# Identity passes on TensorE in the opening and ahead of the last mixer, and ScalarE's, VectorE's and TensorE's steps of the mixers in another order

## The reference

```python
cs = silu(c)
mod = (cs @ ada_w[l] + ada_b[l])                      # 9 x 1024 values for each l
x = x + 0.5 * gate0 * swiglu(norm(x), ...)
x = x + gate1 * mixer(norm(x), ...)                   # convolution + dilated attention, 3 x 8 heads
x = x + 0.5 * gate2 * swiglu(norm(x), ...)
```

```python
q, k, v, xr, xg = split(u @ w_in)
hr = rg_lru(causal_conv(xr), ...)                     # r, ig = sigmoids; a = exp(..); scan over time
y_a = (hr * gelu(xg)) @ w_lru_out
y_b = swa_sink_attention(q, k, v, sinks, bias) @ w_attn_out
g = sigmoid(u @ w_gate + b_gate)                      # two gates, g0 and g1
h = h + norm((g0 * y_a + g1 * y_b) @ w_o)
```

## Time and profile before

| | |
|---|---|
| median of 3 runs | 2094.27 us (2092.14 to 2094.92) |
| the profiled execution | 2095.6 us, of which 2093.5 us are the span of its instructions |
| TensorE matmul / weight load | 2059.9 us (98%) / 1790.4 us (86%) |
| VectorE / ScalarE / GpSimd | 1432.5 us (68%) / 1028.6 us (49%) / 36.3 us (2%) |
| HBM read | 435.05 MB, 208 GB/s over the span |
| granted clock, mean | 0.997 of full speed |

### The profile page before, as it was taken

One profiled execution on the slowest core, in us unless ns is written; L12 is line 12 of the kernel. 1 busy time (PEld: TensorE's weight loads), 2 busy tenths in 40 slices (PEclk: granted clock), 3 DMA queues, 4 the chain that ended last, 5 costly groups with the idle time before them and its releaser, 6 DMA issues.

```text
span 2093.5 us, 28979 instructions
## 1 busy us (share of the span) xinstructions
PE 2059.9 (98%) x11649; PEld 1790.4 (86%) x11649; DVE 1432.5 (68%) x1822; ACT 1028.6 (49%) x1279; POOL 36.3 (2%) x78
## 2 busy tenths in 40 slices
PE   7999999999999999999999999999999999999998
PEld 7788888999888888888899998888788799998887
DVE  5887788668777677767866786455654669656454
ACT  4443544444554363445444445444644668646443
POOL 0000000000000000000000000000000010000000
PEclk9999999999999999999999999999999999999999
DMA  9787698447678748868865496654755454456652
GB/s 316 258 283 251 193 290 253 128 139 253 230 256 267 245 168 277 264 202 260 287 183 145 143 300 192 203 188 141 234 188 183 135 160 137 161 183 210 192 190 80
DMA packets 355929, 438.04 MB, mean 209 GB/s; under 512 B 9571, under 2 KB 323371, under 8 KB 355796
## 3 DMA queue, kind: packets, MB, share of 16 engines
q1 hardware_dynamic: 350592, 420.51, 61.7%
q0 software_dynamic: 4160, 14.23, 3.1%
q10 hardware_dynamic: 1044, 1.46, 0.2%
HBM read 435.05 MB, written 1.11 MB: 208 GB/s over the span
## 4 chain that ended last, share of the span: by engine, by line
PE 88%; DVE 5%; ACT 4%; issue 1%; DMA 1%; DVEq 1%; SPq 0%; ACTq 0%
PE PC L1808 7%; PE PC L1810 7%; PE PC L1809 7%; PE PA L1808 6%; PE PA L1810 6%; PE PA L1809 6%; PE PB L1808 6%; PE PB L1810 6%; PE PB L1809 6%; PE PA L1801 4%; PE PA L1802 4%; PE PA L1803 4%; PE PC L1839 3%; PE PC L1976 2%; PE PC L1801 2%; PE PC L1803 2%
## 5 line engine op out<-in xcount | busy, mean ns | idle before, releaser
L1172 DVE TENSOR_TENSOR lo<-raw,hi 128x2048 fp32r<-128x2048 f32 x274 | 626.7, 2289 | 209.5 <-ACT hi L696 208.4
L696 ACT ACTIVATE hi<-raw 128x2048 fp32r<-128x2048 f32 x277 | 529.3, 1912 | 260.1 <-PE PC L1810 114.8
L1198 DVE SCALAR_TENSOR_TENSOR acc<-raw,cs,acc 128x256 f32<-128x256 f32 x448 | 217.2, 485 | 34.4 <-issue 0.9
L1808 PE MATMUL PA<-hi,nn 128*128 128x512 f32 (+1 forms) x528 | 210.3, 398 | 7.0 <-DVE nn L1274 5.9
L1801 PE MATMUL PA<-nn,hi 128*128 128x256 f32 x720 | 209.0, 290 | 0.4 <-ACT f L1089 0.4
L1810 PE MATMUL PA<-hi,nn 128*128 128x512 f32 (+1 forms) x528 | 206.0, 390 | 0.0
L1809 PE MATMUL PA<-lo,nn 128*128 128x512 f32 (+1 forms) x528 | 205.5, 389 | 0.0
L1802 PE MATMUL PA<-nn,lo 128*128 128x256 f32 x720 | 203.6, 283 | 0.0
L1803 PE MATMUL PA<-nn,hi 128*128 128x256 f32 x720 | 203.6, 283 | 0.0
L1808 PE MATMUL PB<-hi,nn 128*128 128x512 f32 x400 | 158.2, 395 | 0.5 <-DVE nn L1274 0.5
L1810 PE MATMUL PB<-hi,nn 128*128 128x512 f32 x400 | 156.6, 391 | 0.0
(11 more groups left out here) (317 smaller groups left out, 4088.8 us busy)
## 6 DMA issues: line engine op xcount, KB each, us to landing
raw<-in_w_in SPq DMA_DIRECT2D x90, 1024.0 KB, 5.4
raw<-in_ada_w SPq DMA_DIRECT2D x66, 1024.0 KB, 7.4
raw<-in_ffn_w_gate SPq DMA_DIRECT2D x88, 512.0 KB, 4.1
raw<-in_ffn_w_up SPq DMA_DIRECT2D x88, 512.0 KB, 5.2
raw<-in_ffn_w_down SPq DMA_DIRECT2D x44, 1024.0 KB, 5.2
raw<-in_ffn_w SPq DMA_DIRECT2D x88, 512.0 KB, 4.8
raw<-in_ffn_w SPq DMA_DIRECT2D x22, 1024.0 KB, 4.8
raw<-in_w_o SPq DMA_DIRECT2D x12, 1024.0 KB, 6.6
```

Of the source, the lines that this page charges most:

```text
L696: A(parts_of(n)[0], raw[:, n % 3, :], ACT.Copy).then_inc(hi_done, 1)
L1172: V.tensor_tensor(l, raw[:, n % 3, :], h.bitcast(F32), ALU.subtract).then_inc(lo_done, 1)
L1198: i = V.scalar_tensor_tensor(o, w[:, k, :], cs[:, k:k + 1], o, ALU.mult, ALU.add)
L1808: MM(o, xl, wh[:, c0:c0 + w], start=first, stop=False, skip_group_check=True)
```

## The change

- TensorE: a function `warm(n, bank)` multiplies the 128x128 identity by the identity repeated four times (512 columns, fp32), n times, into a bank that nothing reads. In the opening stand 4 behind the first matmul, 3, 1, 1 and 1 in the rounds n = 1, 2, 3 and 4 of the loop over VectorE's five units, and 1 behind `turn_x(0, 1)`, eleven in all; 2 more stand ahead of `values2(0, 7)`, the start of the last mixer.
- TensorE, first-kind mixers: the first scores (j = 0, u = 0) wait for 11 sums of queries and keys instead of all 12, the ones of u = 1 for all 12.
- ScalarE, last mixer: on even hu, `split` comes ahead of `gate2`; the last square root, `lru(3, 1)`, comes behind the split of its hu and ahead of the gate.
- TensorE, last mixer: `first_unit` also waits for `sg_done` 18.
- VectorE: at the change of stage 5 the split comes ahead of `final_norm(0)`; behind the last mixer's loop `lru(3, 3)` comes ahead of `split(b + 19)`.

```diff
--- before.py
+++ after.py
@@ -1137,7 +1137,7 @@
                     recurrent_gates(j)
                 if i == 3 and 1 <= j < 4:
                     lru(j - 1, 2)
-                if i == 0 and j >= 1:
+                if i == 0 and 1 <= j < 4:
                     lru(j - 1, 1)
                 if i == 4 and 0 <= j < 4:
                     lru(j, 0)
@@ -1145,9 +1145,11 @@
                     after(b + 3 + u)
                     if SPREAD[u] == "q":
                         queries(u // 3 + 1, prod[(u + 1) % 2])
-                    elif SPREAD[u] in ("ga", "gc"):
+                    split(b + 6 + u)
+                    if i == 0 and j == 4:
+                        lru(j - 1, 1)
+                    if SPREAD[u] in ("ga", "gc"):
                         gate2(f1 if SPREAD[u] == "ga" else f2, SPREAD[u], 0, prod[1])
-                    split(b + 6 + u)
                 if i == 1 and j == 4:
                     lru(j - 1, 2)
 
@@ -1337,8 +1339,8 @@
                 elif s == 5:
                     add_gated(s, 0)
                     midway()
+                    split(BASE[s + 1])
                     final_norm(0)
-                    split(BASE[s + 1])
                     lows(Aq, 0, (0,))
                     add_gated(s, 1, (0,))
                     lows(Aq, 0, (1,))
@@ -1778,8 +1780,8 @@
                     chunk_T(8 + c, c, oH2, oL2)
 
             def last_chunks():
+                lru(3, 3)
                 split(b + 19)
-                lru(3, 3)
 
             tail(7, TAIL_AT2 + 3, TAIL2[3:], BANK2[3:], gate_home2, mH2, mL2, m322, ya2, False, 8, 19, last_chunks,
                  None)
@@ -2063,6 +2065,15 @@
             pe.wait_ge(const_done, 8)
             pe.wait_ge(c_full, 16)
             MM(PA[:, 512:512 + KC], crow[:, :], ident[0:KC, 0:KC], start=True, stop=True).then_inc(c_turned, 1)
+            wide_ident = bass.AP(ident[:, :].tensor, ident[:, :].offset, [ident[:, :].ap[0], [0, 4], [1, P]])
+
+            def warm(n, bank):
+
+                for _ in range(n):
+                    MM(bank.rearrange("p (e q) -> p e q", e=4), ident[:, :], wide_ident, start=True, stop=True,
+                       skip_group_check=True)
+
+            warm(4, PC[:, 1024:1536])
             pe.wait_ge(cs_done, 1)
 
             def rows_turned():
@@ -2086,15 +2097,22 @@
                     ada_cols_of(1)
                     rows_turned()
                 if n == 1:
+                    warm(3, PC[:, 1024:1536])
                     ada_cols_of(3)
+                if n == 2:
+                    warm(1, PC[:, 1024:1536])
                 if n == 3:
                     turn_x(0, 0)
                     ada_cols_of(6)
+                    warm(1, PC[:, 1024:1536])
+                if n == 4:
+                    warm(1, PC[:, 1024:1536])
                 pe.wait_ge(ada_d, n + 1)
                 for c in (2 * u, 2 * u + 1):
                     i = MM(MOD[:, c:c + 1], acc[:, c * P:(c + 1) * P], ones[:, 0:1], start=True, stop=True)
             i.then_inc(mod_done, 1)
             turn_x(0, 1)
+            warm(1, PA[:, 512:1024])
 
             def bias_lines():
 
@@ -2138,8 +2156,8 @@
                         half(c + u, prod[u], 0, nh, nl)
                         if u == 0 and j:
                             chunk_T(l * 4 + j - 1 if j > 1 else None, (j - 1) % 2, st0 + 4 * j)
-                        if j == 0 and u == 0:
-                            pe.wait_ge(qk_done, 12 * (l + 1))
+                        if j == 0 and u < 2:
+                            pe.wait_ge(qk_done, 12 * l + 11 + u)
                         tick(1, st0, 4 * j, 2 * u, v1, l * 4 + j if j else None)
                         half(c + u, prod[u], 1, nh, nl).then_inc(unit_done, 1)
                         tick(1, st0, 4 * j, 2 * u + 1, v1)
@@ -2167,6 +2185,7 @@
                              k == 0, k == KC - 1)
                 return m
 
+            warm(2, PB[:, 0:512])
             values2(0, 7)
             turn_x(7, 1)
             values2(1, 7).then_inc(unit_done, 1)
@@ -2222,6 +2241,7 @@
 
             def first_unit(k, o):
                 pe.wait_ge(ol_done, 16)
+                pe.wait_ge(sg_done, 18)
                 unit(k, o, oH2, oL2)
 
             def first_recurrent(k, o):
```

## The result

The changed kernel takes **2099.12 us** (median of 7 runs, 2098.70 to 2102.57). The kernel before took 2093.28 us beside it (7 runs, 2092.14 to 2094.92). The ratio is 1.0031 with a 95% interval of 1.0021 to 1.0040, that is 4.4 to 8.4 us slower. The profiled execution took 2099.1 us with a span of 2097.3, against 2095.6 and 2093.5 before: 3.8 us of span.

A forecast was written before the change was run, and what follows sets the result against it. TensorE, 88% of the chain, was taken as the bound: only its idle time or lower clock could matter. Terms 2.0 - 1.3 + 0 - 0.9 + 2.8 + 2.0 = +4.6 on 2094.27 gave 2098.9 us, range 2092.5 to 2105.0.

The forecast's parts named there:

- The opening: Eleven passes in the opening: clock rises, falls in one-column groups, single passes don't restore it; +2.0 us (bounds -0.8, +9.2).
- My mark: Opening: the prediction is wrong if the one-column groups take under 4 us each.
- The first-kind mixers: Earlier first scores remove the 1.08 us key-sum wait; 0.63 us earlier each, twice: -1.3 us (bounds 0, -2.2).
- VectorE's split ahead of the norm: Change of stage 5: norm ends later, but TensorE waits for VectorE a little behind anyway; 0 us (bounds 0, +1.5).
- The two passes: Start of last mixer: they fill a 2.0 us wait and keep the clock; -0.9 us (upper bound +1.9).
- The last mixer's order: ScalarE's new order and first_unit's wait: TensorE idles 5.2 us, partly given back; +2.8 us (bounds +2.0, +3.0).
- The clock behind the idle stretch: Last mixer: TensorE's clock falls behind the 5.2 us without matmuls; +2.0 us (bounds 0, +2.9).
- The carry-over to the median: Whole kernel: the profiled execution lies 1.3 us above its median, so +4.6 was applied to 2094.27 us.
- A: Rival: the clock holds through the opening, -0.8 us there instead of +2.0; total 2096.1 us; chance 0.25.
- B: Rival: fp32 identity passes don't raise the clock, so the opening costs the full +9.2; total 2106.1 us; chance 0.13.
- C: Rival: last mixer's sigmoid is done when TensorE asks (before 1801.4); with the opening at -0.8, 2091.3 us; chance 0.10.
- D: Rival: all gaps and gains over the whole kernel cancel, 2094.3 us; chance 0.05.

The follow-up runs named there:

- experiment 1: Kernel before with only the eleven passes of the opening added: 2096.54 us, ratio 1.0014.
- experiment 5: Changed kernel with TensorE's wait for sg_done 18 moved from first_unit to first_recurrent: 2096.56 us, ratio 1.0009 to the kernel before.
- experiment 7: Kernel before with eight of the opening's eleven passes (4, 3 and the last 1), without the three single ones between: 2094.06 us, ratio 1.0007.
- experiment 8: Kernel before with only the three single passes of the opening, ahead of the last one-column groups: 2097.95 us, ratio 1.0018.
- experiment 4: Kernel before with only the two passes ahead of the last mixer: 2093.79 us, ratio 1.0001.
- experiment 10: Kernel before with only VectorE's two swaps (split ahead of the final norm; lru(3, 3) ahead of split(b + 19)): 2091.97 us, ratio 0.9994.
- experiment 3: Kernel before with only the last mixer's new ScalarE and VectorE order and first_unit's wait for sg_done 18: 2099.88 us, ratio 1.0030.
- experiment 9: Kernel before with only ScalarE's split ahead of the first gate's sigmoid in the last mixer: 2096.10 us, ratio 1.0011.

## Why the prediction was right, and where it wasn't

The forecast was 2098.9 us and the result is 2099.12. That they meet within 0.2 us is partly luck. The forecast was +4.6 on a median of 2094.27; the kernel before had 2093.28 in the comparison, and the change came out at +5.8. And some of the terms were off, in both directions.

**The opening, forecast +2.0.** Line 1216 was to start at 41 and starts at 42.3: +3.4 in the trace, +3.0 in experiment 1. The picture held: the passes at 2.5 us and the three ahead of the second group raise the clock, it falls at such groups (once in the idle stretch behind the first, once inside the second), single passes don't bring it back in this execution, and the last passes are paid in full. The price of a pass held as well: 1.85 us at 1.2 GHz (forecast 1.8), about 0.9 at 2.4 GHz (0.94 for each of the two at 1658.11). What failed is where the clock was high. The three passes ahead of the second group were to end at 20.4 (at 0.9 us each from 18.1 it would be 20.8) and ran at 1.2 GHz to 21.35. Then the second group, which I had half slow (4.5 us), took 3.8 to the next matmul, but from 24.5 on all was slow: the pass at 25.99 took 1.85 instead of 1.4, the third group 6.7 instead of 6.1. (The upper bound is off a little too: its terms add up to 48.3, not 48.) And the step that placed the sum's cost was a choice between -0.8 and +9.2, made without knowing that this cost isn't one number: 0.2 in one execution (experiment 5), 3.4 in another. My mark "wrong if the one-column groups take under 4 us each" was met by two groups of three, and the time came out as forecast nonetheless, since the mark looked at the groups and the cost lies in the single passes (experiments 7 and 8).

**The first-kind mixers, forecast -1.3.** Measured -1.3 in the trace (0.64 and 0.67) and -1.0 by itself. The steps held down to the next wait: 0.7 us on the maximum was forecast, 0.46 measured.

**VectorE's split ahead of the norm, forecast 0.** It is 0: from the second scores of the second mixer to the transposes it is 401.08 us before and 401.06 after.

**The two passes, forecast -0.9.** The trace gives -0.8 against the profiled execution of before, but by themselves they give nothing (experiment 4). The step that failed is to take the 6.8 us fall of the earlier trace rows as a property of the kernel. It is one of that execution; with the usual fall of 3.4 us VectorE is the later one, and nothing is to be gained.

**The last mixer's order, forecast +2.8.** TensorE reaches `first_unit` at 1801.17, 0.85 later against its stretch's start (forecast 0.8). It idles 4.89 (5.2). The waits of 1.42 and 1.23 behind it are gone, as forecast: of the 14.7 us that before took for the two units (1800.62 to 1815.32), 96 matmuls of 0.12 are 11.5, so the waits and the restarts behind them cost 3.2. Then 0.85 + 4.89 - 3.2 = **+2.6**. What I didn't see is that VectorE's swap by itself takes nearly half of those 3.2 away (experiment 10): against the best order of the parts, the wait costs more than the difference of the traces shows.

**The clock behind the idle stretch, forecast +2.0.** The clock fell for 3.4 us. The two units took 13.1 us (1806.06 to 1819.14) where 96 matmuls of 0.12 are 11.5: **+1.6**. With +2.6 it makes the last mixer's +4.1, up to rounding (forecast 4.8). In experiment 3 it fell behind the first sigmoid wait too, which my sum had at nothing and experiment 9 puts at 1.4. Between executions this term is the least certain one.

**The carry-over to the median** hid an error that the others cancelled. The profiled execution of before lies 1.3 us above its median, and its two falls (57.9 and 1658.7) account for 1.6 + 0.8. So what I booked as a gain of the two passes, and the fall at 57.9 that the trace after lacks, are no gains in a comparison of medians. From median to median it is +5.8, from profile to profile +3.5: the forecast of +4.6 lies between. The parts by themselves sum to +3.0 - 1.0 + 6.3 + 0.3 = +8.6; the whole is 2.8 less, of which 1.8 may be the clock at the first gate, which fell in experiment 3's profile and not in after's. Whether it holds for the runs without a profile isn't shown, and each of the four intervals alone reaches about 2 us to either side.

**The rivals.** A (the clock holds in the opening) is refuted by the row at 24.50. B (fp32 passes don't raise the clock) by the row at 9.41: 3.70 us behind four passes. C (the sigmoid is done in time) by the 4.89 us; the condition that I gave, an end before 1801.4, was missed by 4.6 us. D (all cancels) lies outside the ratio's interval.

## What to carry to other kernels

A wait that another engine's last step releases belongs directly ahead of the instruction that overwrites what the step reads; one unit earlier it cost 3.0 us here. With the wait in its place, ScalarE's first gate left alone and one more split of VectorE moved ahead, the last mixer is 3.1 us shorter than before. Of the filler passes on TensorE only those paid that lie in a wait of TensorE longer than they are, with wide matmuls right behind and TensorE as what the end hangs on: five in the 4.9 us wait were worth 2.9 us by the medians and 1.8 by the traces. Two in a wait behind which VectorE was the next late one changed nothing, nor did eight in and around the opening's waits, and three single ones between short groups cost 4.2 by themselves. And before a fall of the clock in one profile is booked as a cost that can be won, look whether another execution has it at the same place and length.

## What the runs showed of the hardware

- A busy TensorE was not enough for the high clock. In after the granted clock stood at 0.50 from 24.50 to 45.00 with TensorE busy for 20.50 of 20.50 us, most of it one-column fp32 matmuls and transposes, with single passes between them. The Trainium skill, TensorE: Matmul & The Clock Gate, section "Why this matters for your kernels", advises to keep TensorE busy and without gaps so that the full rate is reached and stays. Behind the 4.9 us gap the traces agree (a fall there, none when it is filled). In the opening they don't: there is no gap, and the clock stayed at its lower level.
- An fp32 matmul of 128x512 costs 1.85 us from start to start at 1.2 GHz and about 0.94 at 2.4 GHz, and the clock can rise behind such matmuls, as it does behind the wide single-pass ones of the earlier trace rows: the group behind four of them, ahead of which no other wide matmul stands, ran in 3.70 us instead of 6.96.
- Where the clock falls differs from execution to execution of nearly the same instructions. At the small matmuls of `bias_lines` it fell, at 57 to 58 us, in 4 of 14 profiles (25.6 us from line 1216 to the hidden layer's transposes, 24.0 to 24.5 in the other ten), at the start of the last mixer in 10 of 14 (for 3.4 us in eight of them, for 6.8 in two, one of the ten in a kernel with the two passes, of which there are three). A kernel's profile is one draw of these.
